# Output and query projection in two parts: 192 tokens first and gathered, 384 dense

## What is computed

```
x = x + (g_m * a_m + g_f * a_f + g_c * a_c) @ p['w_out']
x = x + peer_ffn(rmsnorm(x, p['norm_ffn']), p['peer_wq'], p['peer_keys'], p['peer_u'], p['peer_v'])

def peer_block(tok, wq, keys, u, v):
    qr = (tok @ wq).reshape(p, PEER_HEADS, 2, PEER_DQ // 2)
    s = jnp.einsum('phcd,hckd->phck', qr, keys)
    top_s, top_i = lax.top_k(s, PEER_TOPK)
    cand = top_s[:, :, 0, :, None] + top_s[:, :, 1, None, :]
    ids = top_i[:, :, 0, :, None] * N_KEYS + top_i[:, :, 1, None, :]
    best, j = lax.top_k(cand.reshape(p, PEER_HEADS, PEER_TOPK * PEER_TOPK), PEER_TOPK)
    eidx = jnp.take_along_axis(ids, j)
    g = jax.nn.softmax(best, axis=-1)
    act = jax.nn.gelu(jnp.einsum('phkd,pd->phk', u[eidx], tok))
    return jnp.einsum('phk,phkd->pd', (g * act), v[eidx])
```

## Time and profile before

| what | us |
|---|---|
| median of three runs | 1951.48 |
| the runs | 1950.44, 1951.48, 1951.83 |
| the profiled execution's own time | 1951.0 |
| its span | 1949.3 |
| output projection | 47.3 |
| query projection | 118.9 |
| U stage | 607.3 |
| gap between U and V | 25.8 |
| V stage | 545.2 |
| end | 17.2 |

### The profile page before, as it was taken

How to read it: one execution, slowest core, us unless ns; L and a number is a source line. 1 busy time by engine, 2 the same in 40 slices (tenths; PEclk the granted TensorE clock), 3 DMA queues, 4 the chain that set the end, 5 groups by cost and what they waited for, 6 DMA issues and landing times.

```text
span 1949.3 us, 34536 instructions
## 1 busy us (share of the span) xinstructions
PE 1888.0 (97%) x12585; PEld 1215.4 (62%) x12596; DVE 1506.5 (77%) x2995; ACT 859.6 (44%) x1313; POOL 941.9 (48%) x586
## 2 busy tenths in 40 slices
PE   9999999999999999999999999998599999999997
PEld 7647777777777776555556666654255555555554
DVE  7975566454355568999899899846798999999885
ACT  6444446555443433333356666642233333333331
POOL 3732222222243353666877777878544445454320
PEclk9999999999999999999999999999799999999998
DMA  5722114223352223777989999999999999999971
GB/s 201 220 100 97 47 55 131 88 86 129 122 155 88 97 77 111 233 271 267 354 281 380 382 378 375 375 326 366 362 379 370 380 394 399 384 400 386 398 284 49
DMA packets 165532, 486.17 MB, mean 249 GB/s; under 512 B 17688, under 2 KB 59744, under 8 KB 164904
## 3 DMA queue, kind: packets, MB, share of 16 engines
q1 hardware_dynamic: 81824, 240.98, 34.4%
q0 software_dynamic: 46208, 167.83, 23.1%
q10 hardware_dynamic: 37384, 75.84, 10.5%
HBM read 419.75 MB, written 64.80 MB: 249 GB/s over the span
## 4 chain that ended last, share of the span: by engine, by line
PE 75%; DVE 14%; POOL 5%; issue 3%; DMA 1%; ACT 1%; ACTq 0%; DVEq 0%; POOLq 0%; SPq 0%
PE ps L2304 27%; PE ps L1847 24%; PE ps L1966 10%; PE ps L1863 3%; POOL w_lo L585 3%; POOL rows L618 3%; DVE rows L1635 2%; PE ps L2120 1%; PE ps L2244 1%; PE ps L2245 1%; DVE eq L1622 1%; DVE eq L1620 1%; PE ps L2100 1%; DVE eq L1619 1%; PE ps L2178 1%
## 5 line engine op out<-in xcount | busy, mean ns | idle before, releaser
L585 POOL TENSOR_TENSOR w_lo<-raw,w_hi 128x1024 bf16<-128x1024 f32 x229 | 503.1, 2201 | 609.6 <-ACT w_hi L695 586.1
L695 ACT ACTIVATE w_hi<-raw 128x1024 bf16<-128x1024 f32 x357 | 374.3, 1051 | 313.8 <-DMA raw<-in_v_units 129.1
L2304 PE MATMUL ps<-W_hi,w_hi 128*128 128x416 bf16 x992 | 337.5, 340 | 25.8 <-DVE W_lo L1771 25.8
L1847 PE MATMUL ps<-act_hi,w_hi 128*128 128x416 bf16 (+1 forms) x1040 | 351.6, 339 | 6.8 <-ACT hb L1055 6.0
L1847 PE MATMUL ps<-act_lo,w_hi 128*128 128x416 bf16 (+1 forms) x1040 | 351.6, 339 | 0.0
L1847 PE MATMUL ps<-act_hi,w_lo 128*128 128x416 bf16 (+1 forms) x1040 | 351.5, 339 | 0.0
L2304 PE MATMUL ps<-W_lo,w_hi 128*128 128x416 bf16 x992 | 337.4, 340 | 0.0
L2304 PE MATMUL ps<-W_hi,w_lo 128*128 128x416 bf16 x992 | 337.4, 340 | 0.0
L618 POOL DMA_INDIRECT rows<-in_v_units,rowi x128 | 170.4, 1331 | 202.1 <-DVE accS L1743 179.8
L1055 ACT ACTIVATE hb<-ps 128x416 f32<-128x416 f32 x128 | 66.2, 517 | 275.9 <-PE ps L1847 261.7
L1721 DVE TENSOR_TENSOR w_lo<-raw,w_hi 128x1024 bf16<-128x1024 f32 x124 | 151.2, 1219 | 43.0 <-ACT w_hi L695 42.9
(11 more groups left out here) (453 smaller groups left out, 3488.4 us busy)
## 6 DMA issues: line engine op xcount, KB each, us to landing
raw<-in_u_units SPq DMA_DIRECT2D x128, 512.0 KB, 5.5
raw<-in_v_units SPq DMA_DIRECT2D x128, 512.0 KB, 10.2
raw<-in_units SPq DMA_DIRECT2D x99, 512.0 KB, 3.3
hd<-hb ACTq DMA_DIRECT2D x128, 224.0 KB, 5.7
Hb<-hd SPq DMA_DIRECT2D x32, 896.0 KB, 8.4
gd<-gsb ACTq DMA_DIRECT2D x48, 448.0 KB, 7.0
Gb<-gd SPq DMA_DIRECT2D x32, 672.0 KB, 6.2
gz<-stage ACTq DMA_DIRECT2D x24, 288.0 KB, 2.1
```

The lines of the kernel that those rows point to most:

```text
L585: pool.tensor_tensor(w_lo[:, k % RING, :], raw[:, k % RAW, :], w_hi[:, k % RING, :], ALU.subtract).then_inc(lo_ready, 1)
L695: act.activation(w_hi[:, k % RING, :], raw[:, k % RAW, :], ACT.Copy).then_inc(hi_ready, 1)
L1847: last = pe.matmul(ps[:, bank + half, 0:n], w[:, slot, col:col + P], x(k)[:, half * n:(half + 1) * n], start=(k == 0 and w is w_hi and x i ...
L2304: ins = pe.matmul(ps[:, d, 0:TDX], w[:, slot, d * P:(d + 1) * P], x[:, k, 0:TDX], start=(first and w is w_hi and x is W_hi), stop=False)
```

## The change

The last 192 tokens (`NA` = 128 + 64) are projected and queried ahead of the other 384 (`TD`). So `w_out` and `peer_wq` are each loaded and split twice (`N_TWICE` = 24 more units), first for 192 columns and then for 384. All 192 are then gathered: `NST` = 128 fetches for the full tile and `NX` = 64 for the half one, now with one list of 192 (`ND`). The half tile lies as two sets of 64 partitions from the start, so the copies between partitions and the tables of their own are gone. The dense part has 384 columns in eight blocks of 48 (`G_BODY` = 6 steps in eight chunks). The G steps start a body earlier (`J_G` = 5). The first gathered tile is routed beside the second half's output tiles (`OUT_AT` names the steps after which a tile's addition stands), six fetches are issued at once when its rows are known, and twelve of its dots stand in the second query projection. In the V stage each second chunk has a second combine. Buffers are laid out anew.

```diff
-TDX = TD - NX
-N_XG = P // 2 // NX
+NX = P // 2
+ND = NST + NX
+T0 = T - NSP
+TD = T0 - NX
+NA = T - TD
-J_G = 6
+J_G = 5
-G_BODY = 7
+G_BODY = 6
-X_FETCH, X_COMB, X_STEP = 113, 8, 3
+DOTS_WQ, DOTS_AT = 12, 4
+FETCH_AT = U_WQ2 + RING - 1
-EARLY_AT = (17, 23, 30, 36)
-DOTS_TWO = 3
+EARLY_AT = (7, 15, 22, 30)
+DOTS_TWO = 4
+OUT_AT = (1, 2, 4, 6, 10, 15, 17, 18)
...
-            for n in range(U_PEER // RAW * RAW, U_PEER):
-                load(a["units"][n], n % RAW, False, n - RAW + 1)
+            for n in range(U_OUT2 // RAW * RAW, U_PEER):
+                load(a["units"][n if n < U_OUT2 else n - N_TWICE], n % RAW, False, n - RAW + 1)
...
+                if n == FETCH_AT:
+                    pool.wait_ge(rows_known, 1)
+                    for s in range(RG):
+                        fetch(s)
+                x = n - (U_WQ2 + RING + DOTS_AT + 1)
+                if 0 <= x < DOTS_WQ:
+                    fetch(RG + x, (dot_done, x + 1))
...
                 if k == EXP_AT:
                     act.wait_ge(tk, (NFT + 1) * N_TK)
...
+            def out_b(j):
+                dve.wait_ge(unit_used, U_OUT2 + j + 1)
+                dve.tensor_tensor(xT[:, j, 0:TD], ps[:, OUT_BANKS[j % 4], 0:TD], xT[:, j, 0:TD], ALU.add).then_inc(x2_ready, 1)
+                if j:
+                    out_low(j - 1)
+                if j >= 2:
+                    add_square_b(j - 1)
...
+            pairs_of(0, NPH, top[:, 0, :, :], topi[:, 0, :, :], topf, abf, eqA, iota16A, tripA[:, :, 0:NST], out_beside)
+            rows_of(slice(0, NST), 1)
+            out_low(KT - 1)
+            add_square_b(KT - 1)
...
-            for s in range(NX):
-                x_dot(s)
...
                 combine(s)
-                i = (s - X_COMB) // X_STEP
-                if s == X_COMB + X_STEP * i and 0 <= i < NX:
-                    x_combine(i)
+                if s % 2:
+                    x_combine(s // 2)
...
-                tile(n % RING, lambda k: mg_hi[:, k, :], lambda k: mg_lo[:, k, :], 2 * (j % 2),
+                tile(n % RING, lambda k: mg_hi[:, k, mA], lambda k: mg_lo[:, k, mA], j % 2, n=NA, halves=1,
                      ready=None if j else 0, split=g_mlo).then_inc(unit_used, 1)
...
+            for j in range(KT):
+                n = U_OUT2 + j
+                pe.wait_ge(lo_ready, n + 1)
+                if j == 2:
+                    pe.wait_ge(tk1, 4 * NHC)
+                if j >= 4:
+                    pe.wait_ge(x2_ready, KT + j - 3)
+                tile(n % RING, lambda k: mg_hi[:, k, mB], lambda k: mg_lo[:, k, mB], OUT_BANKS[j % 4], n=TD,
+                     halves=1).then_inc(unit_used, 1)
...
-                tile((U_PEER + k) % RING, a_hi, a_lo, k % 2, n=TDX, halves=1).then_inc(unit_used, 1)
+                tile((U_PEER + k) % RING, lambda x: h_hi[:, x, :], lambda x: h_lo[:, x, :], k % 2, n=TD, halves=1).then_inc(unit_used, 1)
```

More of the change, by code:

```diff
@@ L1076, in two_bodies @@
                             act.wait_ge(b_written[b], it * (PIECES * 16))
-                        if k and not (last and b == 1 and k > G_LAST):
+                        if 1 <= k <= G_BODY:
                             s, at = b * G_BODY + k - 1, (k - 1) * GT
@@ new lines, in out_beside @@
+            def out_beside(step):
+                if step in OUT_AT:
+                    out_b(OUT_AT.index(step))
+            pairs_of(0, NPH, top[:, 0, :, :], topi[:, 0, :, :], topf, abf, eqA, iota16A, tripA[:, :, 0:NST], out_beside)
+            rows_of(slice(0, NST), 1)
+            out_low(KT - 1)
+            add_square_b(KT - 1)
+            dve.wait_ge(n_rms, 4)
+            dve.reciprocal(rB[:, 1, :], rB[:, 0, :]).then_inc(n_inv, 1)
+            for q in range(NHC):
+                dve.wait_ge(s_ready, NHC + q + 1)
+                top16(step1, lambda x: ps[:, 4 + q % 2, x * P:(x + 1) * P], lambda x: rest[:, x, :],
+                      lambda x: top[:, 1 + x, q, :], lambda x: topi[:, 1 + x, q, :], NFT - 1)
+                if 0 <= q - DOTS_AT < DOTS_WQ:
+                    dot(q - DOTS_AT)
@@ L2211, in _ @@
                     pe.wait_ge(q_evac, q - 1)
-                tile(n % RING, *xg, 2 * (q % 2), ready=None if q else 2 * KT).then_inc(unit_used, 1)
+                tile(n % RING, lambda k: xg_hi[:, k, mA], lambda k: xg_lo[:, k, mA], 2 + q % 2, n=NA, halves=1,
+                     ready=None if q else 2 * KT).then_inc(unit_used, 1)
+                if q == 0:
+                    token_sums_a()
+                if q == 1:
+                    token_rows_a()
+                    pe.wait_ge(keys_in, 16)
@@ new lines, in _, with turn_tokens @@
+                if q:
+                    key_scores_a(q - 1)
+            key_scores_a(NHC - 1)
+            def turn_tokens():
+                pe.wait_ge(h_scaled, KT)
+                pe.wait_ge(half_kept, NHC)
+                pe.wait_ge(q_evac, NHC)
+                for x in range(KT):
+                    last = pe.transpose(ps[:, 6 + x // 4, x % 4 * P:(x % 4 + 1) * P], hA[:, x, NX:NA], ident[:, :])
+                last.then_inc(tok_turned, 1)
+                for b in range(2):
+                    for x in range(KT):
+                        last = pe.matmul(ps[b * HP:(b + 1) * HP, 2 + x // 4, x % 4 * P:(x % 4 + 1) * P], hA[:, x, 0:NX],
+                                         ident[:, :], start=True, stop=True)
+                last.then_inc(x_turned, 1)
@@ new lines, in key_scores, with token_sums @@
+            def key_scores(q):
+                pe.wait_ge(q_evac, NHC + q + 1)
+                if q >= 2:
+                    pe.wait_ge(tk1, 4 * (NHC + q - 2) + 2)
+                for t in range(NFT - 1):
+                    last = pe.matmul(ps[:, 4 + q % 2, t * P:(t + 1) * P], qrB[:, q % 2, t * P:(t + 1) * P], keys[:, q, :],
+                                     start=True, stop=True)
+                last.then_inc(s_ready, 1)
+            def token_sums():
+                pe.wait_ge(n_add, (KT - 1) * 4)
+                for t in range(NFT - 1):
+                    last = pe.matmul(ps[:, 0, t:t + 1], sqB[:, 0, t * P:(t + 1) * P], ones[:, 0:1], start=True, stop=True)
+                last.then_inc(n_ssq, 1)
@@ new lines, in token_rows @@
+            def token_rows():
+                pe.wait_ge(n_inv, 4)
+                for t in range(NFT - 1):
+                    last = pe.matmul(ps[:, 1, t * P:(t + 1) * P], rB[:, 1, t:t + 1].broadcast_to((P, P)), ident[:, :], start=True,
+                                     stop=True)
+                last.then_inc(r2_spread, 1)
+            pe.wait_ge(x2_ready, 2 * KT)
+            pe.wait_ge(x_kept, 1)
+            for q in range(NHC):
+                n = U_WQ2 + q
+                pe.wait_ge(lo_ready, n + 1)
+                if q >= 2:
+                    pe.wait_ge(q_evac, NHC + q - 1)
+                tile(n % RING, lambda k: xg_hi[:, k, mB], lambda k: xg_lo[:, k, mB], 2 + q % 2, n=TD, halves=1,
+                     ready=None if q else 3 * KT).then_inc(unit_used, 1)
@@ L2395 @@
     ])
-    assert units.shape == (U_PEER, P, 1024)
+    assert units.shape == (U_PEER - N_TWICE, P, 1024)
     par = np.zeros((P, N_PAR), f32)
```

573 lines of the change are left out of this document (292 added, 281 removed).

## The result

The changed kernel takes **2059.15 us** (median of four runs, 2045.66 to 2069.96), the kernel before 1950.96 (median of four, 1949.81 to 1951.83). The ratio is 1.0551, interval 1.0481 to 1.0622: 5.5% slower. The forecast was 1936, its range 1908 to 1968. The profiled run's own time is 2069.96 and its span 2068.2, 118.9 us over the span before.

The account below looks back on a forecast made before the run. Bound by back-to-back matmuls in U and V. Query stage +16, U −21, gap −2 and V −8 sum to −15: span 1949.3 to 1934, forecast time 1936 us, range 1908 to 1968.

Parts of the forecast that it names:

- Four resources between 35 and 40 us: I take 39: U's G blocks: TensorE, VectorE, GpSimd and DMA need similar times, so 39 us a block, for 40.2 before.
- 2.3 above TensorE: U's G blocks: each block of 39 us exceeds TensorE's own 36.7 by 2.3, 18 us over eight.
- VectorE 4.0 … I take 4.15, nearer the demand that was met than the ends: V stage: VectorE needs 4.0 us a chunk, DMA 3.98 to 4.22; 4.15 taken, V −8 in all.
- full-DMA rival: DMA full at 385 GB/s: V at 4.30 us a chunk, 1969 us in all, slower than before; chance 0.18.
- The rival's other terms: Full DMA outside V: six G blocks that write gd at 39.8 us (+6), tail and gap +8.
- Forecast +16: Output and query stage: from 166 to 182 us, range +6 to +28.
- TensorE waits some 6 us: Query stage, part B: last low half stands behind the first tile's routing; wait 6 us, 0 to 12.
- 60 forecast: Part A, output and query projection of the first 192 tokens: 60 us of TensorE time, with 3.1 for waits and norm.
- the ring of units: Output and query stage: 24 extra units cost 0, up to 8 us if dry; dry-ring rival 1946 us, chance 0.05.
- this same lock: VectorE and GpSimd's shared port pair, cited for the rival of later routing at U's start: +14, 1950 us, chance 0.16.
- 18 forecast: Early U: TensorE stands some 18 us near chunk 31, as the exponentials wait for VectorE's routing.
- It starts with slack, so I count no stop there: U's tail, 24 chunks of two fetches: GpSimd 4.5 us a chunk and more against TensorE's 3.90, no stop counted.

Follow-up runs that it names:

- e1: Changed kernel with the gathers for the dots of the G blocks and tail two chunks earlier in GpSimd's order: 1987.78 us.
- e3: Changed kernel with G-block gathers and those for V's second combine cut to one-row copies, output not the reference's: 1962.15 us.
- e6: e1 with V's second combine on 8 of 1024 columns and U's exponentials at chunk 31 instead of 29: 1980.79 us.
- e5: e1 with GpSimd's low halves, from the output projection to chunk 39 of U, on 8 of 1024 columns: 1961.72 us.
- e10: e1 with the exponentials at chunk 31 instead of 29, whole computation: 1986.82 us.

## Why the prediction was wrong

**G blocks.** The step that failed is "Four resources between 35 and 40 us: I take 39". It asked how busy each engine would be and never how long the way is from a gather's place in GpSimd's order to its use. What the list left out was a fifth entry, the lead of the gathers. The runs show it in its place: with nothing but the gathers two chunks earlier, the eight blocks fall from 407.6 to 321.9 us, and the run by 71 of the miss of 123. The 39 came near the 40.2 that a block then takes in the mean, but this is in part luck: four of these blocks take 36.7, TensorE's own time, with all four resources at work, and the others 39 to 50, so "2.3 above TensorE" in every block for nearly full engines is not what happens. The numbers for the lead were in the order and in the trace: four to six chunks before, two to five after, and the 17 dots that waited up to 1.0 us for their rows in the G blocks of the kernel before said that little of the lead was left over.

**V.** "VectorE 4.0 … I take 4.15, nearer the demand that was met than the ends": measured 4.23 and, in e1, 4.32 a chunk. The full-DMA rival had this term right (4.30 at 385 GB/s); e3 and e6 speak for DMA and against VectorE. The rival's other terms were not right, since the G blocks reach 408 GB/s in e1. With the end, V gave +7 for a forecast −8.

**Output and query stage.** Forecast +16, measured +33. B was right in kind: "TensorE waits some 6 us" for the routing was 9.5. It ended with VectorE's last addition, 45 us after A, and not with the last low half; the row numbers stood 48 us after A for my 47 to 48. The term that was mis-sized is part A, 60 forecast and 73.0 measured. I had counted the ring of units at 0 and looked at TensorE alone. VectorE's two operations a tile, held under GpSimd's low halves, do not hide behind a tile of 2.0 us as they did behind one of 5.9. I had weighed this same lock for the routing and not asked where else the tiles had become short. The waits are 8 us for the 3.1 counted. The granted clock is 0.5 for 10.2 us of part A (0.93 in its mean): a stretch of 3.4 us that begins 1 us after a wait of 2.3, and one of 6.8 that begins inside a wait of 2.4; at half the clock that costs some 5 us, an estimate. And a query tile of part A is repeated every 2.70 us, not 2.56, another 2 us over 16 tiles that I had counted too low.

**U's start.** Right: TensorE stopped 16.3 us for the exponentials (18 forecast), at chunk 31. The cause was only half right, since in e5, with GpSimd's low halves cut, there is no stop at all.

**U's tail and gap.** "It starts with slack, so I count no stop there" failed. 24 chunks of two fetches took 111.4 us from the last G step where TensorE needs some 98, GpSimd busy 95 of the last 111: its 4.5 us a chunk, which I had worked out, is the likeliest pace; no run tests it, and TensorE's waits there (10.1 us) are for gelu, with ScalarE waiting for unit loads and hd writes. In return the gap was 19 for 24, and 7.0 in e1. Tail and gap together are 130.5 for my 122.

**Matmuls.** Right for the dense part: 24 of 384 columns in 3.90 us, a block without waits in 36.7.

What stays open: why a lead that is some 6 us short costs 11 us a block; why the runs of the changed kernel spread over 24 us and those of the kernel before over 2 to 10 (a loop of waits may well do that, but no run shows it); and why V takes 4.32 a chunk in e1, 4.37 in e10 and 4.23 in the changed kernel at the same volume.
